# A hybrid streaming encoder step on one core: the clears of the overflow rows are issued tile by tile in the recurrence, and two gate matrices get a semaphore each

## What is computed

```
p  = rms_norm(h) @ w_in              # one combined projection, 1024 -> 4864
hq, hf, hv, hg, aq, ak, av, ga, gb = split(p)
o_rec = hgrn2_scan(q, k, v, log f)   # gated linear recurrence, 4 heads of 128 x 128
o_att = attend(...)                  # sliding window attention
y_rec = rms_norm(o_rec, gain) * silu(hg)
h  = h + (sig(ga) * (y_rec @ Wb_a) + sig(gb) * (o_att @ Wb_b)) @ W_out
h  = h + moe(rms_norm(h))            # 32 experts, top 2; each token's two rows are added
```

## Time and profile before

| | us |
|---|---|
| median of 3 runs | 2148.14 |
| the runs | 2147.24 to 2150.05 |
| the profiled execution | 2148.96 |
| its span in the trace | 2147.3 |
| PE busy in the span | 1783.2 (83%) |
| mean granted TensorE clock | 0.909 of full speed |
| POOL busy in the span | 95.4 (4%) |

### The profile page before, as it was taken

The page is one execution under the profiler, slowest core; times in us unless marked ns, Lnnn a source line. Parts: engine busy times, 40 slices in busy tenths (PEclk is TensorE's granted clock), DMA queues, the critical chain, the costliest instruction groups (busy, mean ns, idle before and its releaser), DMA issues. The chain is left out here.

```text
span 2147.3 us, 23818 instructions
## 1 busy us (share of the span) xinstructions
PE 1783.2 (83%) x9270; PEld 860.2 (40%) x9270; DVE 566.2 (26%) x1122; ACT 453.3 (21%) x1011; POOL 95.4 (4%) x115
## 2 busy tenths in 40 slices
PE   7899995888875599899959999946989889889980
PEld 3344743555543245555534454433323223223220
DVE  2111201677763123223212222232110010011004
ACT  2153201243331234334310001000111011011110
POOL 0000002000030000000000000001000000000003
PEclk9999997999997789989969999976999999999995
DMA  4310005111124600100025123156899999999947
GB/s 129 98 60 30 30 20 187 74 49 44 39 74 139 212 28 25 49 24 25 34 104 188 73 103 117 49 185 237 330 406 352 351 399 347 345 390 356 336 196 289
DMA packets 123181, 350.18 MB, mean 163 GB/s; under 512 B 14360, under 2 KB 37952, under 8 KB 121808
## 3 DMA queue, kind: packets, MB, share of 16 engines
q1 hardware_dynamic: 102352, 282.86, 35.8%
q0 software_dynamic: 11840, 42.47, 5.4%
q10 hardware_dynamic: 8912, 23.74, 2.8%
HBM read 288.61 MB, written 53.36 MB: 159 GB/s over the span
## 5 line engine op out<-in xcount | busy, mean ns | idle before, releaser
L1963 PE MATMUL ps<-ring,xsT 128*32 128x512 f32 x3072 | 336.9, 595 | 1.4 <-DVE xsT L1922 1.4
L1982 PE MATMUL ps<-ring,hT 128*32 128x512 f32 x1536 | 185.6, 643 | 55.0 <-DMA ring<-w_expert_down 54.7
L1289 PE MATMUL ps<-wg,xt 128*128 128x512 f32 x432 | 209.1, 640 | 14.1 <-DMA xt<-xn_dram 9.0
L1963 PEld LDWEIGHTS ps<-ring,xsT 128*32 128x32 f32 x3072 | 97.3, 110 | 223.7 <-issue 221.9
L261 PE MATMUL ps<-wbuf,wide 128*128 128x512 f32 (+3 forms) x464 | 171.2, 529 | 9.3 <-issue 9.3
L256 PE MATMUL ps<-wide,wbuf 128*128 128x512 f32 (+1 forms) x384 | 130.8, 504 | 11.3 <-issue 11.3
L1289 PEld LDWEIGHTS ps<-wg,xt 128*128 128x128 f32 x432 | 86.2, 205 | 127.9 <-issue 111.3
L1566 PE MATMUL ps<-wb,mt 128*128 128x512 f32 x288 | 128.4, 599 | 10.8 <-DMA mt<-wide 8.5
L1589 PE MATMUL ps<-wo,mgT 128*128 128x512 f32 x288 | 128.9, 601 | 3.0 <-DVE logits L1533 3.0
L1982 PEld LDWEIGHTS ps<-ring,hT 128*32 128x32 f32 x1536 | 52.5, 117 | 175.8 <-issue 175.8
L261 PEld LDWEIGHTS ps<-wbuf,wide 128*128 128x128 f32 (+1 forms) x464 | 86.4, 189 | 87.0 <-issue 81.1
(11 more groups left out here) (327 smaller groups left out, 1820.4 us busy)
## 6 DMA issues: line engine op xcount, KB each, us to landing
ring<-w_expert_gate SPq DMA_DIRECT2D x32, 2048.0 KB, 24.0
ring<-w_expert_up SPq DMA_DIRECT2D x32, 2048.0 KB, 23.3
ring<-w_expert_down SPq DMA_DIRECT2D x32, 2048.0 KB, 25.4
y_dram<-au ACTq DMA_DIRECT2D x24, 512.0 KB, 9.8
y_dram<-wide POOLq DMA_DIRECT2D x46, 256.0 KB, 9.0
gt<-g_dram SPq DMA_DIRECT2D x9, 1024.0 KB, 6.0
wbuf<-w_in SPq DMA_DIRECT2D x8, 1024.0 KB, 5.7
g_dram<-gb SPq DMA_DIRECT2D x9, 768.0 KB, 3.3
```

Of the source, the lines that this page charges most:

```text
L1289: last = pe.matmul(ps[2][:, :], xt[:, k * P:(k + 1) * P], wg[:, j, k, :], start=(k == 0), stop=(k == KC - 1))
L1963: last = pe.matmul(bank[r][member(a), :], xsT[:, q % 2, r, k, member(a)], ring[:, n % RING, a, h * FF:(h + 1) * FF], start=(k == 0), stop= ...
L1982: last = pe.matmul((psx, psy)[c][r][member(a), :], hT[:, r, k, member(a)], ring[:, n % RING, a, c * 512:c * 512 + 512], start=(k == 0), st ...
```

## The change

It does three things, all in `recur`:

- `whg` and `wgt` count on semaphores of their own, `s_whg` and `s_wgt`. PE waits for `s_xt` at 16 i + 16 (xt alone) and for `s_whg` in front of the first L767 of a tile, and for `s_wgt` in front of the eight matmuls with `wgt`.
- The loop that clears 14 blocks at the stage's start is gone.
- The clears are issued behind `scale_gate` of the first eight tiles: three blocks (six transfers) behind each of tiles 0 to 6, and the last two blocks (four transfers) behind tile 7. Behind the tile ST none is left. It is 23 blocks as before.

```
+        s_whg = m.sem("r_whg")
+        s_wgt = m.sem("r_wgt")
 ...
-            sp.dma_start(whg[:, :, :], w_in[:, :, C_HG:C_HG + HW]).then_inc(s_xt, 16)
-            sp.dma_start(wgt[:, :, :], w_in[:, :, C_GB + 512:C_GB + D]).then_inc(s_xt, 16)
+            sp.dma_start(whg[:, :, :], w_in[:, :, C_HG:C_HG + HW]).then_inc(s_whg, 16)
+            sp.dma_start(wgt[:, :, :], w_in[:, :, C_GB + 512:C_GB + D]).then_inc(s_wgt, 16)
 ...
             pool.memset(zero, 0.0)
             pool.drain()
-            with pool.Fori(NMAIN + NT, NBLK) as b:
-                clear(b)
             pool.wait_ge(s_const, RCONST)
 ...
             def scale_gate(i):
                 ...
-                clear(i + NMAIN)
-
-            with pool.Fori(0, PT) as i:
+
+            with pool.Fori(0, PT - 1) as i:
                 scale_gate(i)
+                for b in range(OVER // (PT - 1)):
+                    clear(i + NMAIN + b * (PT - 1))
+            scale_gate(PT - 1)
+            for b in range(OVER // (PT - 1) * (PT - 1), OVER):
+                pool.dma_start(T.y_dram[NMAIN + b, :, 0:HW], zero).then_inc(s_zw, 16)
+                pool.dma_start(T.y_dram[NMAIN + b, :, HW:], zero).then_inc(s_zw, 16)
 ...
                     if l == 0:
-                        pe.wait_ge(s_xt, 16 * i + 48)
+                        pe.wait_ge(s_xt, 16 * i + 16)
+                        pe.wait_ge(s_whg, 16)
                         pe.wait_ge(s_sg, i + 1)
 ...
                 if levels < LEVELS:
                     pe.wait_ge(s_sn, H)
+                pe.wait_ge(s_wgt, 16)
                 gate_matmuls(psg, wgt, range(0, KC // 2), s_gj)
```

## The result

The changed kernel takes 2133.15 us in the median of 4 runs (2132.85 to 2134.28), the kernel before 2147.69 us beside it: a ratio of 0.9936, 95% interval 0.9918 to 0.9954. It is faster by 14.5 us and not by the 22.7 that were forecast, and 2133.15 lies above the stated range, whose end was 2131.5.

The account below looks back on a forecast made before the run. The bound was PE's 21.7 us idle wait for `wgt` at the recurrence's start, while DMA engines were full. Terms -21.5 - 0.9 + 0.3 + 0.4 - 1.0 = -22.7 us gave 2125.4 us; range 2122.5 to 2131.5.

Parts of the forecast that it names:

- the stall at the start: PE's 21.7 us wait before tile 0's first `whg` matmul shrinks to 0.2 us: -21.5 us.
- the clock behind it: Tile 0 after the wait: PE reaches full clock sooner as its work is unbroken; -0.9 us, bounds 0 and -1.8.
- the clears inside the tiles, one more wait: Tile loop: clears behind `scale_gate` cost 0; a second wait before L767 costs +0.3 us, at most eight times 0.14.
- the end of tile 7 and the streams' tile: Two terms: POOL's products delayed by two more issues, +0.4 us; no clears beside the streams' state loads, -1.0 us.
- The end of the eight tiles: Behind tile 7: two more issues start POOL's products 0.8 to 1.2 us later, delaying DVE; +0.4 us, between 0 and +1.2.
- The last clear: Streams' tile: two clears no longer share the DMA engines with the state loads; -1.0 us, between 0 and -1.3.
- the bound of 13.4: Late bound for `whg` at the start: landing 13.4 us after issue, like next-stage loads; 3.9 us wait.
- the rivals by which they do: Clears delay `xt` in the tiles: two in each of seven, 2134 us, chance 0.05; all six, 2152 us, chance 0.03.

Follow-up runs that it names:

- e1: The changed kernel, with one block of clears (two transfers) behind tile 7 and the last block behind the streams' tile; 2131.85 us, ratio 0.9911.
- e5: The kernel before with only the two semaphores for `whg` and `wgt`, all clears where they were; 2136.28 us, ratio 0.9936.
- e4: The kernel before with one of the start's 14 cleared blocks moved behind tile 7, so four transfers there; 2155.19 us, ratio 1.003.
- e3: The changed kernel with POOL's four products for the streams issued behind the gate of the streams' tile; 2128.97 us, ratio 0.9898.
- e7: The changed kernel with a drain behind each of POOL's four products; 2130.01 us, ratio 0.9904.
- e9: The changed kernel measured again, with no edit; 2137.74 us, ratio 0.995.
- e6: The changed kernel with one semaphore for `xt`, `whg` and `wgt` again, so only the clears are moved; 2140.96 us, ratio 0.9963.
- e10: e3 with PE's matmuls with `whg`, and the waits for them, moved behind level 1 instead of level 0; 2108.4 us, ratio 0.9809.

## Why the prediction was wrong

Term by term, from the two profiles:

| term | forecast | measured |
|---|---|---|
| the stall at the start (0.25 of it ahead of the stage) | -21.5 | -20.6 |
| the clock behind it | -0.9 | 0.0 |
| the clears inside the tiles, one more wait | +0.3 | +0.2 |
| the end of tile 7 and the streams' tile | +0.4 - 1.0 | +7.4 |
| later stages | 0 | -2.7 |
| sum | -22.7 | -15.7 |

**The step that failed** is "The end of the eight tiles". It saw the right place and even the right sign: POOL's products 0.8 to 1.2 us later (measured: 0.75, from 0.77 behind the start of the state's update to 1.52), and DVE's steps with two operands that wait for them. But it priced the delay as a shift, at +0.4 and at most 1.2 us, as if DVE's share in the row of products stayed what it was; with the state loads the end of the stage cost 7.4 us. It argued from one step, L668 with 2.38 us, which takes 0.67 in the changed kernel; the step that is held there is the product of `sq` and the gate ahead of it, L725 before and L730 after. What changed was where DVE's step falls in the row. In the kernel before, as in e1 and e5, the step comes 1.92 us behind the start of the products and passes behind the second (two products of 1.86 us end at 621.34, the step at 621.91); 0.75 us of delay for POOL bring it to 1.17 to 1.19 us, inside the first product, and then it isn't let in until the fourth has ended. That more transfers in the queue ahead of the products bring the loss about is shown by e1 and e4, that it needs the products and their unbroken row by e3 and e7, and that it repeats by e9 and e6. Whether the time of the step decides, or that the products follow on a transfer without a wait, is not shown: in all eight profiles of an undrained row in this place the two go together.

The Trainium skill, SBUF — State Buffer, "Who interferes with whom", states that a VectorE instruction with two inputs in SBUF contends with a GpSimd instruction that reads SBUF, that the shared ports are an exclusive lock, and that the order of issue decides who blocks. The rows agree on who contends: L730 reads `sq` and the gate from SBUF and is held, while L725 and L727, with an operand in PSUM, run in 0.68 and 0.69 us beside the first product. On the order they differ, and the measurement decides: the step starts at 599.12, 0.7 us before the second product, and still waits for the second, third and fourth (6.83 us; one product is 1.86).

The term also left out what a late step causes further on. PE's pause of 7.47 us cost another 2 us in clock, and the late `xt` 2.58 us of wait where there had been none. That the measured time misses the forecast by no more than 7.0 us on the profile is in part luck: 2.7 us came from the later stages, where the forecast and the change had nothing.

**The last clear** beside the loads of the state, -1.0 in the sum, gave nothing. From the first of these loads to PE's product it took 636.76 to 647.05 = 10.3 us before and 624.47 to 634.92 = 10.45 after; in e1, where a block is cleared there again, 10.3. From 643 to 645 us, as the clears were issued, 290 GB/s moved, and 289 in the same stretch of the changed kernel (631 to 633); only in the 2 us behind it do they differ, 356 against 88 GB/s, and these 536 thousand bytes are about the clears' 524. So the clears moved when the loads had little left to move, and the sharing that the prediction read from the landing of 4.4 us did not delay them.

**The stall** was mis-sized by 0.9, and by 1.2 without the 0.25 that lay ahead of the stage: `whg` landed 10.6 us after issue, between the forecast's 8.9 and the bound of 13.4. The rate was not the reason. The changed kernel's stretches from 348 us on:

```profile
348.00:350.00 2.00, 0.60 (x4) 0.28 (x4) 0.71 (x2) 1.03 (x3) 0.52 (x1) 1.00 0.84 247
350.00:352.00 2.00, 1.72 (x9) 1.50 (x10) 0.72 (x2) 0.23 (x1) 0.00 (x0) 0.68 0.63 168
352.00:354.00 2.00, 2.00 (x9) 1.70 (x9) 2.00 (x5) 1.23 (x2) 0.00 (x0) 0.50 1.01 375
354.00:356.00 2.00, 0.93 (x5) 0.72 (x4) 2.00 (x5) 1.00 (x3) 0.00 (x0) 0.50 1.05 402
356.00:358.00 2.00, 1.81 (x9) 1.52 (x8) 1.76 (x5) 0.53 (x2) 0.00 (x0) 0.50 1.05 392
358.00:360.00 2.00, 0.56 (x4) 0.27 (x3) 1.17 (x3) 1.19 (x3) 0.00 (x0) 0.50 1.05 387
```

By 358 us 3168 thousand bytes had moved, and all that is queued up to the end of `whg` is 3215: the bytes are where the forecast has them, at 358.3. But `xt` landed only at 354.1 (1118 thousand are queued up to its end, and 1580 had moved by 354), and `whg` at 359.8, when some 3850 thousand had moved. The 600 thousand too many can only be `wgt`, the one load behind `whg`. So the step that failed in this term is that `whg` has the DMA engines to itself until it lands: a load behind it on the same queue moves before it has landed. Whether `wgt` issued later would let `whg` land sooner was not tried. Without clears beside it, `whg` landed 9.8 to 11.5 us after issue in nine profiles; with them, in e5, after 16.3.

**The clock** gave nothing back: as PE did wait 1.44 us for `whg`, its work was broken there, and it came up 4 to 5 us later, as before. Tile 0 took 379.11 - 359.99 = 19.12 us against 19.13.

**What held.** The clears inside the tiles met no `xt`: the rivals by which they do are out, by the step of 30.77 us. The 42 issues in the tiles took 0.54 us in the median, at most 0.76. The Trainium skill's 3.1 us for one beside VectorE (SBUF — State Buffer, as cited in the prediction) shows in none of them. The wait on one semaphore more was at most 0.02 us a tile.

## What to carry to other kernels

When an edit moves work on one engine by a microsecond, look for the other engine's steps that wait for it, and ask what such a step would have to wait out, not how much later it comes: here 0.75 us of delay made one step wait for a whole row of four instructions. A long row of POOL products like this one belongs where VectorE waits for something else (e3), or needs a break between them (e7). And a transfer that is issued just in time on a chain that repeats eight times is worth more than a stall at its start: moving two matmuls behind the next level (e10) gave some 19 us on top of e3 by the two ratios, more than the change itself.

## What the runs showed of the hardware

- DVE's two-operand step beside POOL's four products, `sq` and the gate, has two outcomes in eight profiles of the undrained row: 2.37 us, when it came 1.92 us behind their start (three profiles), or 6.30 to 6.84, ending behind the last product, when it came 1.17 to 1.70 us behind (five); in the ninth, with a drain between the products, it was 1.28. Why a step that came during the first product isn't let in behind it, while one that came during the second is, stays open. In the three profiles in which it passed, a wait released the products, and in the five in which it was held they followed on a transfer; no run separates that from the time at which the step came. Once a step has passed, the two engines take turns: in the kernel before, DVE's next step (L682, at 622.38) came during the third product and ended at 624.22, before the fourth, which ended at 625.97.
- The granted clock of TensorE fell to 0.50 in some pauses and not in others of the same length: after 3.02 us in e1 and 3.00 in e5, not after 3.01 us in the kernel before. A tile step of 31.7 to 32.6 us instead of 30.8 stands in none to three tiles of a profile; in long tiles of e1, e3, e4 and e7 the clock was below full speed for some 3 us of PE's work. Runs of one kernel lay up to 11 us apart; how much of that is this, and how much the later stages, was not measured.
